# A hybrid encoder trunk on one NeuronCore: the backward output matrix of the S5 layer built by GpSimd instead of VectorE, with earlier parameters and scratch elsewhere

## What is computed

```python
lam_bar = jnp.exp(lam * dt)
b_bar = ((lam_bar - 1.0) / lam)[..., None] * b_mat
bu = jnp.einsum('bsgc,gpc->sbgp', ug, b_bar)
_, states = lax.associative_scan(_linear_combine, (a, bu), axis=0, reverse=(d == 1))
y = y + jnp.real(jnp.einsum('sbgp,gcp->bsgc', states, c_mat)).reshape(B, S, S5_WIDTH)
```

## Time and profile before

| quantity | value |
|---|---|
| median of three runs | 1696.32 us (1693.79 to 1696.9) |
| the profiled execution's own time | 1700.06 us |
| its span, first to last instruction | 1698.1 us |
| mean granted clock of PE | 0.981 |
| busy: PE, DVE, ACT, POOL | 94%, 39%, 26%, 18% of the span |
| chain that ended last: PE, DVE, DMA | 85%, 7%, 4% |

### The profile page before, as it was taken

One profiled execution on the slowest core, in us unless ns is written; L12 is line 12 of the kernel. 1 busy time (PEld: TensorE's weight loads), 2 busy tenths in 40 slices (PEclk: granted clock), 3 DMA queues, 4 the chain that ended last, 5 costly groups with the idle time before them and its releaser, 6 DMA issues.

```text
span 1698.1 us, 20387 instructions
## 1 busy us (share of the span) xinstructions
PE 1598.4 (94%) x8292; PEld 837.2 (49%) x8292; DVE 653.8 (39%) x1200; ACT 438.3 (26%) x778; POOL 301.1 (18%) x374
## 2 busy tenths in 40 slices
PE   8999979979999999999799999898899999999986
PEld 4654656555444444443357546555554444444422
DVE  1695565451211221221428846664512212222115
ACT  3564730311111111111235657202111111111112
POOL 5460770000000000000364409500000000000003
PEclk9999999989999999999999999999999999999997
DMA  7000303659999999999930021065699999999996
GB/s 316 1 1 15 135 1 86 277 221 382 401 429 427 428 427 428 428 428 427 370 139 1 1 83 67 1 185 237 258 360 424 427 429 427 428 428 428 427 428 237
DMA packets 56721, 468.77 MB, mean 276 GB/s; under 512 B 17809, under 2 KB 17937, under 8 KB 30098
## 3 DMA queue, kind: packets, MB, share of 16 engines
q1 hardware_dynamic: 44578, 443.23, 63.1%
q10 hardware_dynamic: 9744, 15.80, 2.5%
q0 software_dynamic: 2304, 8.39, 1.4%
HBM read 446.42 MB, written 18.88 MB: 274 GB/s over the span
## 4 chain that ended last, share of the span: by engine, by line
PE 85%; DVE 7%; DMA 4%; ACT 2%; issue 1%; another core or an unknown queue 0%; POOL 0%; POOLq 0%; SPq 0%; DVEq 0%
PE bank L875 24%; PE bank L869 12%; PE bank L905 12%; PE bank L544 11%; PE bank L680 5%; DMA ring<-wu 4%; PE bank L853 2%; PE bank L619 2%; PE bank L634 2%; PE bank L606 2%; PE bank L538 2%; PE bank L892 1%; PE bank L515 1%; PE bank L722 1%; DVE ring L1549 1%
## 5 line engine op out<-in xcount | busy, mean ns | idle before, releaser
L875 PE MATMUL bank<-ring,hbuf 128*64 128x512 f32 x704 | 312.6, 598 | 16.0 <-DMA ring<-wu 13.4
L876 PE MATMUL bank<-ring,hbuf 128*64 128x512 f32 x704 | 312.8, 598 | 0.0
L1784 DVE COPY raw_qd<-bank 128x256 f32<-128x256 f32 x64 | 27.2, 425 | 714.5 <-PE bank L892 714.5
L2029 POOL DMA_INDIRECT raw_qd<-expert_rows,dest_i x12 | 11.7, 978 | 1161.6 <-DMA expert_rows<-raw_qd 1158.5
L544 PE MATMUL bank<-hbuf,ring 128*128 128x512 f32 x480 | 210.0, 594 | 0.0
L869 PE MATMUL bank<-raw_qd,x 128*128 128x256 f32 x896 | 207.3, 385 | 0.0
L875 PEld LDWEIGHTS bank<-ring,hbuf 128*64 128x64 f32 x704 | 96.5, 138 | 215.3 <-issue 215.3
L869 PEld LDWEIGHTS bank<-raw_qd,x 128*128 128x128 f32 x896 | 165.9, 190 | 24.0
L905 PE MATMUL bank<-ring,raw_qd 128*64 128x512 f32 x352 | 160.5, 598 | 5.2 <-DVE raw_qd L1784 4.7
L907 PE MATMUL bank<-ring,raw_qd 128*64 128x512 f32 x352 | 160.5, 598 | 0.0
L1259 ACT ACTIVATE raw_qd<-bank 64x512 f32<-64x512 f32 x64 | 37.8, 591 | 414.8 <-PE bank L876 414.8
(11 more groups left out here) (359 smaller groups left out, 2253.7 us busy)
## 6 DMA issues: line engine op xcount, KB each, us to landing
ring<-wg SPq DMA_DIRECT2D x44, 2048.0 KB, 17.6
ring<-wu SPq DMA_DIRECT2D x44, 2048.0 KB, 20.9
ring<-wd SPq DMA_DIRECT2D x44, 2048.0 KB, 19.4
ninth_slot<-wd SPq DMA_DIRECT2D x20, 2048.0 KB, 19.4
hbuf<-wu SPq DMA_DIRECT2D x20, 2048.0 KB, 20.9
raw_qd<-wg SPq DMA_DIRECT2D x20, 2048.0 KB, 16.2
ring<-w_in SPq DMA_DIRECT2D x8, 2048.0 KB, 15.0
expert_rows<-raw_qd ACTq DMA_DIRECT2D x120, 128.0 KB, 8.8
```

What stands on the lines that cost most here:

```text
L875: mm(pb[2 + par][0:CAP, :], tokens[:, k, :], gates[:, k, :], start=(k == 0), stop=(k == KT - 1))
L876: last = mm(pb[2 + par][CAP:P, :], tokens[:, k, :], ups[:, k, :], start=(k == 0), stop=(k == KT - 1))
```

## The change

- `s5_b` is loaded first in SP's queue, after the wait for the four k v products, with a semaphore of its own (`s5b`); `s5_c` keeps its place; w_out waits for `o_a` (both pairs normalised) instead of `ho`.
- Pool waits for `s5b` and for the end of rotary work before it prepares b; for `s5p` only before A3; for `q_silu` instead of `o_a` before BtT; for `state` before Ct_f. It builds Ct_b itself, after Ct_f, and signals `ct`; it waits for `ho` before the decay rows.
- DVE's three passes for Ct_b go; DVE and ACT wait for `ct` before their first copy of Bt.
- `s_tmp` moves to ring tile 1, A1 and A2 to ring tile 0, `o_sb` and `o_rs` to ring tiles 5 and 4, `n_sb` within ring tile 1. A rotary step on DVE waits by `link` instead of by a semaphore of its own.

The diff, without the lines that only rename or recount semaphores:

```diff
--- before.py
+++ after.py
@@ -158,8 +158,9 @@
         SCAN = 512
         dec_sb = [ring[:, 4, 1024 + SCAN * i:1024 + SCAN * i + SCAN] for i in range(2)]
         hg_t = [ring[:, 2, 512 * i:512 * i + 512] for i in range(2)]
-        o_sb = [ring[:, 2, 1536 + 512 * i:2048 + 512 * i] for i in range(2)]
-        o_rs = [ring[:, 2, 2560 + 512 * i:3072 + 512 * i] for i in range(2)]
+        o_keep = ring[:, 5, 1026:2050]
+        o_sb = [o_keep[:, 512 * i:512 * i + 512] for i in range(2)]
+        o_rs = [ring[:, 5, 3074:3586], ring[:, 4, 2048:2560]]
 
         rope_sq = [ring[:, 1, 2562 + 512 * i:3074 + 512 * i] for i in range(2)]
         rope_t = ring[:, 1, 2050:2562]
@@ -186,15 +187,15 @@
 
         S5 = ring[:, 1, 0:DG * NK].rearrange("p (d k) -> p d k", d=DG)
         Y5 = raw[:, 1024:2048].rearrange("p (t g c) -> p t g c", t=SC, g=G5 // 2)
-        s_tmp = ninth[:, 1024:3328]
+        s_tmp = ring[:, 1, 1026:3330]
         gt = [hbuf[:, 512 * i:512 * i + 512] for i in range(4)]
         yT = [tile(raw, 512 * i) for i in range(2)]
 
         Wr = gB[:, 320:320 + NPOW * DG].rearrange("p (i d) -> p i d", i=NPOW)
         Wi = gB[:, 608:608 + NPOW * DG].rearrange("p (i d) -> p i d", i=NPOW)
         W_t = gB[:, 896:1024].rearrange("p (i d) -> p i d", i=4)
-        A1 = ninth[:, 3328:3616].rearrange("p (i d) -> p i d", i=NPOW)
-        A2 = ninth[:, 3616:3904].rearrange("p (i d) -> p i d", i=NPOW)
+        A1 = ring[:, 0, 2304:2592].rearrange("p (i d) -> p i d", i=NPOW)
+        A2 = ring[:, 0, 2592:2880].rearrange("p (i d) -> p i d", i=NPOW)
         A3 = hbuf[:, 5408:5696].rearrange("p (i d) -> p i d", i=NPOW)
         A4 = hbuf[:, 5120:5408].rearrange("p (i d) -> p i d", i=NPOW)
         ss = [gB[:, 32 * i:32 * i + 32] for i in range(10)]
@@ -398,7 +399,7 @@
         E_BANK, H_BANK, KV_BANK = pb[4], (pb[5], pb[6]), (pb[4], pb[5], pb[6], pb[7])
         O_BANK, M_BANK = pb[7], (pb[4], pb[5])
         S_BANK, T_BANK, A_BANK = (0, 2), 4, (pb[6], pb[7])
-        n_sb = [ring[:, 1, 3072 + P * i:3200 + P * i] for i in range(2)]
+        n_sb = [ring[:, 1, 3584 + P * i:3712 + P * i] for i in range(2)]
 
         def sync_program(sp, layer):
             s, on = of_layer(layer)
@@ -406,6 +407,8 @@
             if layer == 0:
                 sp.dma_start(ybuf[LATE * CAP:NROWS], raw[0:1, 8192:9216]).then_inc(s_zeroed, 16)
 
+            sp.wait_ge(s["kv"], on("kv") + HG)
+            sp.dma_start(s5_b, s5p[layer, :, 0:1024]).then_inc(s["s5b"], 16)
             wait_evacuated(sp, layer, 24)
             wait_evacuated(sp, layer, 25)
             for i in range(2):
@@ -417,9 +420,7 @@
 
             sp.wait_ge(s["pe"], on("pe") + NG)
             sp.dma_start(s5_c, s5p[layer, :, 1024:2048]).then_inc(s["s5p"], 16)
-            sp.wait_ge(s["kv"], on("kv") + HG)
-            sp.dma_start(s5_b, s5p[layer, :, 0:1024]).then_inc(s["s5p"], 16)
-            sp.wait_ge(s["ho"], on("ho") + 2)
+            sp.wait_ge(s["o_a"], on("o_a") + 2)
             for i in range(2):
                 sp.dma_start(ring[:, 4 + i, :], w_out[layer, i]).then_inc(slot[4 + i], 16)
 
@@ -1183,6 +1184,7 @@
                     probs(u + 2)
 
 
+            act.wait_ge(s["ct"], on("ct") + 1)
             for q in range(1, 8, 2):
                 act.wait_ge(s["bt"], on("bt") + q + 1)
                 A(flat(Bt[:, 4 * q:4 * q + 4, :]), pb[q % 6][:, :], ACT.Copy).then_inc(s["bt_e"], 1)
@@ -1407,8 +1409,7 @@
             def rope_turn(j):
                 dve.wait_ge(s["r_y"], on("r_y") + j + 1)
                 link(V.stream_shuffle(rope_t, rope_x[j], PAIRS))
-                TT(rope_t, rope_t, cst("sin"), ALU.mult).then_inc(s["r_t"], 1)
-                dve.wait_ge(s["r_t"], on("r_t") + j + 1)
+                link(TT(rope_t, rope_t, cst("sin"), ALU.mult))
                 link(TT(rope_x[j], rope_x[j], cst("cos"), ALU.mult))
                 link(TT(rope_x[j], rope_x[j], rope_t, ALU.add))
 
@@ -1532,24 +1533,9 @@
                 residual(n, pb[6 + n % 2], n + 1)
 
 
-            dve.wait_ge(s["pv"], on("pv") + NU)
-            dve.wait_ge(s["bc"], on("bc") + 1)
-            back = slice(G5, DG)
-            ct_b = Ct_b
-            ct_t = ring[:, 3, 0:G5 * NPOW * C5].rearrange("p (d i c) -> p d i c", d=G5, i=NPOW)
-            c_re, c_im = (s5_c[:, DG * C5 * i:DG * C5 * i + DG * C5].rearrange("p (d c) -> p d c", d=DG) for i in range(2))
-
-            def power(w):
-                return w[:, ::-1, back].rearrange("p i d -> p d i")[:, :, :, None].broadcast_to([P, G5, NPOW, C5])
-
-            def value(v):
-                return v[:, back, :][:, :, None, :].broadcast_to([P, G5, NPOW, C5])
-
-            TT(ct_b, power(A3), value(c_re), ALU.mult)
-            link(TT(ct_t, power(A4), value(c_im), ALU.mult))
-            TT(ct_b, ct_b, ct_t, ALU.add).then_inc(s["ct"], 1)
             early(0)
             early(1)
+            dve.wait_ge(s["ct"], on("ct") + 1)
             for q in range(0, 8, 2):
                 dve.wait_ge(s["bt"], on("bt") + q + 1)
                 V.tensor_copy(flat(Bt[:, 4 * q:4 * q + 4, :]), pb[q % 6][:, :]).then_inc(s["bt_v"], 1)
@@ -1975,7 +1961,9 @@
             link(TT(pv_fi, pv_fi, pv_den, ALU.mult))
 
 
-            pool.wait_ge(s["s5p"], on("s5p") + 32)
+            pool.wait_ge(s["s5b"], on("s5b") + 16)
+            pool.wait_ge(s["r_done"], on("r_done") + 5)
+
             d3 = lambda ap: ap.rearrange("p (d c) -> p d c", d=DG)
             b_re, b_im, c_re, c_im = (d3(ap[:, DG * C5 * i:DG * C5 * i + DG * C5]) for ap in (s5_b, s5_c) for i in range(2))
             fr, fi = (a[:, :, None].broadcast_to([P, DG, C5]) for a in (pv_fr, pv_fi))
@@ -1991,6 +1979,8 @@
             for to, a_, b_, sub in ((A1, ("is_re", Wr), ("is_im", Wi), False), (A2, ("is_im", Wr), ("is_re", Wi), True),
                                     (A3, ("is_re", Wr), ("is_im", Wi), True), (A4, ("is_im", Wr), ("is_re", Wi), False)):
                 t = s_tmp[:, 0:NPOW * DG]
+                if to is A3:
+                    pool.wait_ge(s["s5p"], on("s5p") + 16)
                 link(TS(w2(to), w2(a_[1]), cst(a_[0]), None, ALU.mult))
                 link(TS(t, w2(b_[1]), cst(b_[0]), None, ALU.mult))
                 link(TT(w2(to), w2(to), t, ALU.subtract if sub else ALU.add))
@@ -2009,11 +1999,15 @@
             forward, backward = slice(0, G5), slice(G5, DG)
             t8 = s_tmp[:, 0:G5 * SC * C5].rearrange("p (d i c) -> p d i c", d=G5, i=SC)
             t9 = s_tmp[:, 0:G5 * NPOW * C5].rearrange("p (d i c) -> p d i c", d=G5, i=NPOW)
-            pool.wait_ge(s["o_a"], on("o_a") + 2)
+            pool.wait_ge(s["q_silu"], on("q_silu") + 4)
             link(times(BtT[:, forward, :, :], forward, 0, SC, True, A1, A2, b_re, b_im, t8))
             times(BtT[:, backward, :, :], backward, 0, SC, False, A1, A2, b_re, b_im, t8).then_inc(s["bc"], 1)
             pool.wait_ge(s["bc"], on("bc") + 1)
+            pool.wait_ge(s["state"], on("state") + 4)
             times(Ct_f, forward, 0, NPOW, False, A3, A4, c_re, c_im, t9).then_inc(s["bc"], 1)
+            pool.wait_ge(s["bc"], on("bc") + 2)
+            times(Ct_b, backward, 0, NPOW, True, A3, A4, c_re, c_im, t9).then_inc(s["ct"], 1)
+            pool.wait_ge(s["ho"], on("ho") + 2)
             link(G.tensor_copy(rho, pv_rho8[:, :, None].broadcast_to([P, DG, NK])))
             G.memset(rho[:, :, 0], 0.0).then_inc(s["rho"], 1)
 
```

More of the change, by code:

```diff
@@ L249, in trunk @@
         names = dict(
-            s5p="S5 parameters loaded", h="Pool: diagonal of the inverse root mean squares of a block",
+            s5p="S5 output parameters loaded", s5b="S5 input parameters loaded", h="Pool: diagonal of the inverse root mean squares of a block",
             pe="PE: h^T and projection groups", ev_d="DVE: groups evacuated", ev_a="ACT: groups evacuated",
@@ L258, in trunk @@
             r_sq="ACT: rope squares", r_y="DVE: rope gained tile", r_pe="PE: rope sums",
-            r_ln="ACT: rope log mean squares", r_t="DVE: rope swapped rows times sines", r_rs="ACT: rope rstd", r_done="DVE: rope tile done",
+            r_ln="ACT: rope log mean squares", r_rs="ACT: rope rstd", r_done="DVE: rope tile done",
             ke_t="PE: k_end transposed", ke_e="ACT: k_end^T evacuated", hs_pe="PE: HGRN scores",
@@ L269, in trunk @@
             ang="Pool: S5 angles, denominators",
-            bc="Pool: S5 Bt^T, then forward Ct", ct="DVE: S5 backward Ct", tab="Pool: S5 rotations for 32 chunks, then for all",
+            bc="Pool: S5 Bt^T, then forward Ct", ct="Pool: S5 backward Ct", tab="Pool: S5 rotations for 32 chunks, then for all",
             kp="PE: S5 kernels of a bank", ke="S5 kernels evacuated", kdiag="DVE: S5 kernel diagonal",
@@ L292, in trunk @@
         PER_LAYER = dict(
-            u_out=32, u_in=128, s5p=32, m5=240, pe=26, ke_t=4, hs_pe=4, kv=4, r_pe=5, ho=2, qk=16, ho_m=2,
+            u_out=32, u_in=128, s5p=16, s5b=16, m5=240, pe=26, ke_t=4, hs_pe=4, kv=4, r_pe=5, ho=2, qk=16, ho_m=2,
```

(6 more changed lines are left out.)

## The result

| | before | changed |
|---|---|---|
| median of four runs | 1696.61 us | 1683.72 us (1682.82 to 1686.62) |
| profiled execution, span | 1700.06, 1698.1 | 1683.77, 1681.8 |
| mean granted clock of PE | 0.981 | 0.985 |

The ratio is 0.9916, 95% interval 0.9899 to 0.9934: 12.9 us less between the medians. Measured again later, beside a median of 1695.49 of the kernel before, the same changed kernel gave 0.9941 (0.9928 to 0.9954). The forecast was 15.65 us less and 1680.7. The measured time lies within its range up to 1687; of the likelier part, 1677.5 to 1684.5, the first median lies inside and the second (1685.05) just outside.

What follows compares the result with a forecast made beforehand. The bound was taken to be the mixers' chain through DVE's backward Ct passes after attention. Gains of 7.35 and 8.3 us, other parts 0, make 15.65 off 1700.06: 1684.4, or 1680.7 as median; range 1677.5 to 1684.5, wider to 1687.

Steps and rivals of the forecast that it cites:

- Part 1: Layers 1 and 2, after attention: backward Ct's 17.3 us leave DVE, TensorE's gap closes; gain 7.35 and 8.3 us.
- Part 2: Pool's preparation, its B half landing at 155.4, ends backward Ct at 236.6, wanted at 241.6; cover 5.0 us.
- Part 3: w_out's load issued later, at 186.5, landing at 199.6 to 201, wanted at 230.34; cost nothing, 29 us of cover.
- Part 4: Pool earlier beside DVE before attention: four DVE instructions 3.8 us longer, within 7.47 idle; cost 0 to about 0.5 us.
- Pool just too late: C half stays behind u, DVE slows preparation, ct near 245; each layer gains about 4 us: 1688.5; chance 0.10.
- Pool much too late: All twelve large Bt and Ct passes go slowly, ct at 266.6; each layer loses 18 us: 1732; chance 0.04.
- Absorbed: Expert stage's transfers, ready at a time not set by the mixer, wait the gain away: 1696; chance 0.05.

Runs made afterwards that it cites:

- backward Ct back on DVE: The changed kernel with the removed backward Ct passes restored on DVE behind the last attention unit; 1685.01 us, ratio 0.9935 to the kernel before.
- early B half alone: The kernel before with only the B half loaded early (Pool's wait split, rope step linked), backward Ct still on DVE; 1685.43 us, ratio 0.9942.
- B half late again: The changed kernel with the load of the B half put back behind that of the C half; 1698.38 us, ratio 1.001 to the kernel before.
- DVE waits for Pool: The kernel before, with DVE beginning backward Ct only when Pool has finished forward Ct; 1699.8 us, ratio 1.0019.

## Why the prediction was right, and where its reasons were not

The place and the size were right: both gaps of 5.54 us closed, the clock stayed at 1.00, and the stretch shrank by 7.3 and 8.8 us where 7.35 and 8.3 were forecast. The reason given for it, that the work must leave DVE, was not what gave the time, and between the medians less was gained than in the stretches.

- **Part 1, the cause.** The step that failed is "Its 17.3 us in each layer lie wholly between attention's end and the first Bt copy", read as work that must leave DVE. It is 7.7 us of work; the rest was the meeting with Pool, which ran until 245. Once Pool starts early, the passes may stay on DVE and cost nothing ("backward Ct back on DVE", "early B half alone"). I had taken DVE's company out of Pool's 7.24 (rightly: the addition took 5.05 to 5.09 without it) and had not taken Pool's out of DVE's 5.80 and 7.33, though a 512-column product of 0.69 in the earlier trace rows gives about 3.1 for 2304 columns in proportion, and 2.55 was measured. That this error did not reach the number is luck: with the work off DVE its price there no longer counted.
- **Part 2, Pool's timing.** The last k v product ended at 150.85 + 1.12 = 151.97 and Pool started 4.1 us later; forecast 4.7 (the issue took 0.36 us, where 0.2 was put without a row, and the half landed 3.9 us after it, not 4.5). The pause for the C half, the order and the cover held. The additions were sized 0.7 to 0.8 us too long each, for the distance of the operands.
- **Part 3.** Right; w_out was issued 3.1 us later than worked out, with no effect.
- **Part 4.** The cover of 7.47 us held. What was missed is the head norm, for which the sum has no term, only its old length in part 3: Pool's long passes now begin among the norms instead of 13 us after them. The row of 1.65 us was beside Pool's short operations; beside a long one it is 4.25. It cost 0.6 us in layer 1, just above the 0 to 0.5 of the forecast. The Trainium skill, "SBUF — State Buffer", section "Who interferes with whom", calls the port pair that the two engines share an exclusive lock: the one that comes second is blocked, not slowed. This trace agrees: 185.31 to 189.56 is the rest of Pool's pass from 184.90, then 0.7 us of its own.
- **Rivals.** "Pool just too late" did not come true here, but "B half late again" shows its mechanism and its price: 7 us late, 7.5 to 9.2 us more in each stretch. "Pool much too late" did not come true: beside attention Pool's passes took 3.8 to 4.4 us, and where long passes met in the kernel before, they took turns, so that the 7.24 of its row is 5.05 and a wait. "Absorbed" is out as a whole; that the gain was passed on whole is not borne out either (below).
- **The size at the end.** The stretches give 16.1 us, the spans 16.3, the medians 12.9 and, measured again, 10.4. The spans are two single executions, and that of before lies 3.4 above its median, that of the changed kernel on it. From the last down product (L905, now L906) to its end the one of before took 25.3 us and the changed one 23.0, and the eight others lie anywhere from 22.6 to 27.3. One part of what the medians lack may lie in the first expert stage, from its first selection product (L853, now L854) to the start of layer 2. It took 490.7 us before and 492.5 after. Here the traces show a pattern: the clock is at 0.50 when the selection products start, and comes back sooner or later in them. Stretches of 2 us, the third one behind the first selection product, before and after:

```profile
355.69:357.69 2.00, 2.00 (x20) 1.00 0.01 4
349.46:351.46 2.00, 2.00 (x12) 0.56 0.00 0
```

In four traces the clock is back 3.9 to 4.3 us after the first selection product (before, backward Ct on DVE, B half late again, DVE waits for Pool), and the stage takes 490.6 to 490.8 us. In the other six it is back 5.7 to 6.2 us after it, and the stage takes 492.1 to 493.0. The first 64 selection products account for about half of that (9.27 us before, 10.15 after). Four traces are few, and both groups hold kernels with and without the gain, so whether this is what takes 3 to 6 us of the 16.1 from the medians stays open; no run tests it.

## What to carry to other kernels

A pass that looks long on VectorE beside a busy GpSimd must be priced alone before it is moved: here 17.3 us were 7.7. One early 512 KB load, which let GpSimd finish before VectorE's turn, gave the whole gain that a change of engine, four groups of moved scratch and new waits gave. When long GpSimd passes are moved in time, look at each two-input VectorE instruction that they will now meet, not only at those at the old place. And a late matrix is paid twice, as idle time of TensorE and as its low clock behind it.

## What the runs showed that I had not expected

- GpSimd's addition over 2304 columns takes 5.03 to 5.09 us or 4.26, over 2048 columns 4.53 or 3.82, by a shift of one operand by two columns (8 bytes); the products over 2048 columns with a broadcast operand take 3.88 either way.
- A GpSimd copy over 2048 columns takes 4.22 us beside VectorE's long products and 1.89 without them.
- A VectorE instruction of 0.69 us took 4.25 behind one GpSimd pass of 3.88.
- Long passes of the two engines that meet take turns, one whole pass each: the 17.3 us of three VectorE passes were 7.7 of work.
